# One matmul operand of an expert-mixing kernel moves by 192 bytes in the on-chip memory

## The reference, cut to what matters

```python
act = gelu(einsum('td,tkd->tk', x, u[e]))
out = einsum('tk,tkd->td', g * act, v[e])
```

## Time and profile before

| what | value |
|---|---|
| time, median of 3 runs | 1453.61 us (1453.2 to 1453.62) |
| profiled execution: span, first to last instruction | 1448.3 us |
| profiled execution: its own time | not recorded beside the span; the median is 5.3 us above the span |
| TensorE busy | 1414.5 us, 98% of the span, 7503 matmuls |
| weight loads | 1233.1 us, 85% |
| VectorE busy | 1236.6 us, 85% |
| ScalarE busy | 587.7 us, 41% |
| GpSimd busy | 557.0 us, 38% |
| moved by DMA | 402.34 MB, mean 278 GB/s |

### The profile page before, as it was taken

How to read it: one execution, slowest core, us unless ns; L and a number is a source line. 1 busy time by engine, 2 the same in 40 slices (tenths; PEclk the granted TensorE clock), 3 DMA queues, 4 the chain that set the end, 5 groups by cost and what they waited for, 6 DMA issues and landing times.

```text
span 1448.3 us, 20679 instructions
## 1 busy us (share of the span) xinstructions
PE 1414.5 (98%) x7503; PEld 1233.1 (85%) x7503; DVE 1236.6 (85%) x2019; ACT 587.7 (41%) x693; POOL 557.0 (38%) x389
## 2 busy tenths in 40 slices
PE   7999999999999999999999999999999999999997
PEld 6775478899999999898888888888888888888886
DVE  6988969999999988656788888888898888888889
ACT  3561363333335787753333333333333333333331
POOL 0100224559964000001445545454465555554500
PEclk7899999999999999999999999999999999999999
DMA  9824340025566789898999999999999999999961
GB/s 381 324 117 174 145 193 1 1 76 177 185 216 209 246 251 275 272 341 331 371 367 346 370 365 356 368 354 369 358 361 379 368 359 360 377 363 366 355 228 58
DMA packets 159326, 402.34 MB, mean 278 GB/s; under 512 B 11392, under 2 KB 79104, under 8 KB 156192
## 3 DMA queue, kind: packets, MB, share of 16 engines
q1 hardware_dynamic: 120688, 262.17, 51.2%
q0 software_dynamic: 38288, 139.08, 25.4%
q10 hardware_dynamic: 288, 0.29, 0.1%
HBM read 359.56 MB, written 41.94 MB: 277 GB/s over the span
## 4 chain that ended last, share of the span: by engine, by line
PE 66%; DVE 24%; DMA 4%; ACT 3%; issue 1%; SPq 1%; DVEq 0%; ACTq 0%
PE bank L983 21%; PE bank L984 21%; PE bank L985 20%; DMA u_raw<-ut_dram 2%; DVE arena L1598 2%; DVE arena L1590 2%; DMA wbuf<-ada_w_dram 2%; DVE arena L1595 1%; DVE arena L1587 1%; DVE arena L1639 1%; DVE arena L1592 1%; DVE arena L1640 1%; PE bank L1072 1%; DVE arena L1636 1%; PE bank L1196 1%
## 5 line engine op out<-in xcount | busy, mean ns | idle before, releaser
L983 PE MATMUL bank<-h_lo,u_hi 128*128 128x384 f32 (+1 forms) x1256 | 438.7, 349 | 1.4 <-POOL u_lo L617 1.2
L985 PE MATMUL bank<-h_hi,u_hi 128*128 128x384 f32 (+1 forms) x1256 | 433.2, 345 | 0.0
L984 PE MATMUL bank<-h_hi,u_lo 128*128 128x384 f32 (+1 forms) x1256 | 433.1, 345 | 0.0
L984 PE MATMUL bank<-v_hi,w_lo 128*128 128x512 f32 x744 | 294.5, 396 | 0.0
L983 PE MATMUL bank<-v_lo,w_hi 128*128 128x512 f32 x744 | 292.1, 393 | 0.3 <-DVE w_lo L1736 0.3
L985 PE MATMUL bank<-v_hi,w_hi 128*128 128x512 f32 x744 | 290.4, 390 | 0.0
L983 PEld LDWEIGHTS bank<-h_lo,u_hi 128*128 128x128 f32 x1256 | 236.1, 188 | 14.1 <-issue 2.0
L984 PEld LDWEIGHTS bank<-h_hi,u_lo 128*128 128x128 f32 x1256 | 236.2, 188 | 11.3 <-issue 0.5
L877 ACT ACTIVATE v_hi<-v_raw 128x2048 fp32r<-128x2048 f32 x62 | 119.0, 1919 | 312.4 <-PE bank L985 301.8
L985 PEld LDWEIGHTS bank<-h_hi,u_hi 128*128 128x128 f32 x1256 | 236.0, 188 | 9.4
L1730 DVE TENSOR_TENSOR v_lo<-v_raw,v_hi 128x2048 fp32r<-128x2048 f32 x62 | 142.8, 2304 | 110.2 <-ACT v_hi L877 108.7
(11 more groups left out here) (246 smaller groups left out, 1814.6 us busy)
## 6 DMA issues: line engine op xcount, KB each, us to landing
u_raw<-ut_dram SPq DMA_DIRECT2D x128, 512.0 KB, 6.1
v_raw<-v_dram SPq DMA_DIRECT2D x64, 1024.0 KB, 7.3
gate_in<-gates_dram SPq DMA_DIRECT2D x64, 384.0 KB, 7.2
wbuf<-ada_w_dram SPq DMA_DIRECT2D x6, 2048.0 KB, 11.1
early_dram<-arena SPq DMA_DIRECT2D x64, 192.0 KB, 2.1
gates_dram<-wbuf SPq DMA_DIRECT2D x3, 4096.0 KB, 16.3
w_raw<-early_dram SPq DMA_DIRECT2D x64, 192.0 KB, 5.5
wbuf<-ada_w_dram SPq DMA_DIRECT2D x8, 1024.0 KB, 15.8
```

Source lines behind the costliest of these rows:

```text
L983: pe.matmul(out, a_hi, b_lo, start=(k == 0), stop=False)
L984: pe.matmul(out, a_lo, b_hi, start=False, stop=False)
L985: return pe.matmul(out, a_hi, b_hi, start=False, stop=(k == n - 1))
```

## The change

`gap1` grows by 48 floats and `gap2` shrinks by 48. `w_lo` between them begins 192 bytes further up; all behind `gap2` stays in place.

```diff
         w_hi = sb("w_hi", [P, 2, 2, SD], F32R)
-        sb("gap1", [P, 720])
+        sb("gap1", [P, 768])
         w_lo = sb("w_lo", [P, 2, 2, S], F32R)
-        sb("gap2", [P, 816])
+        sb("gap2", [P, 768])
```

## The result

| | before | changed | ratio, 95% interval |
|---|---|---|---|
| first comparison, median us | 1453.57 (5 runs) | 1445.65 (5 runs, 1443.53 to 1447.15) | 0.9946 [0.9934, 0.9958] |
| second comparison (first experiment), median us | 1450.82 (19 runs) | 1446.76 (8 runs) | 0.9972 [0.9960, 0.9983] |
| profiled executions, span us | 1448.3 and 1447.2 | 1443.9 and 1442.5 | |

Of twelve further runs of the kernel before (`again_before`) one took 3242.77 us, which no ratio here counts and nothing here explains. What the change did is best seen in the loop of 60 pairs, which is the same to 0.01 us in both profiles of each kernel.

What follows compares the result with a forecast made beforehand. TensorE's matmul steps were taken to bound the loop: 60 value blocks, each 0.15 us shorter (8.32 to 8.17), save 9.0 us, so 1453.6 - 9.0 = 1444.6 us; range 1443.8 to 1447.8.

Steps and rivals of the forecast that it cites:

- TensorE is the bound, and stays it: In the loop everybody waits for TensorE; its pair goes from 12.48 to 12.33 us, VectorE has at most 10.8 us.
- The rival on transfers: DMA engines, 0.98 to 0.99 busy, become the bound at 368 GB/s; only 1.8 us gained, 1451.8 us; chance 0.03.
- The settled step falls from 231.1 to 226.7 ns: Value matmuls of 512 columns in the loop: with w_lo at the common place, 36 steps take 8.16 us.
- no change: Rival: the value step depends on something else, such as traffic, or tiles are placed otherwise; 1453.6 us; chance 0.06.
- slower: Rival: coinciding starts of weights and stream cost time; value steps rise to 233.3 ns, 1458.4 us; chance 0.05.
- Start-up price 0.01 us per value block: First steps after the 384-column expert matmuls cost 0.01 us extra, so a block takes 8.17 us and gains 0.15.
- the nearest row: Last two pairs' matmuls after the loop, all operands at the common place, settled after three steps; basis for 9.0 us.
- the lower bound of 6.0: Gain if each value block's first 12 steps stay and only the other 24 shorten: 0.10 us per block, 6.0 us.
- The gain arrives whole: What the 60 value blocks save reaches the end whole, since the closing chain leaves TensorE with the gelu at 1397.82 us.
- 5.3 us lie around the span: Measured median 1453.61 us is 5.3 us above the profiled span of 1448.3; the change does not affect that.

Runs made afterwards that it cites:

- first experiment: Kernel before and changed kernel run once more, files unchanged: medians 1450.82 us (19 runs) and 1446.76 us (8 runs), ratio 0.9972.
- again_before: The kernel before, run again with nothing changed: median 1450.37 us over all 12 runs, ratio 0.9999 to the kernel before.
- the wide kernel: Changed kernel with the expert matmuls of 48 pairs over 512 token columns instead of 384, the added columns not read: 1505.69 us.

## Why the prediction was right, and which term was off

- *TensorE is the bound, and stays it.* Right: no wait in the loop after but the 0.3 us at its start, at 367 and 372 GB/s. The rival on transfers is refuted; 368 was no ceiling.
- *The settled step falls from 231.1 to 226.7 ns.* Right, with 5.44 us for 24 steps. The rival "no change" fell with it, and "slower" too: of eight places of the weights, none has shorter steps than the one where starts coincide.
- *Start-up price 0.01 us per value block.* This is the term that was mis-sized. It is 2.76 - 2.72 = 0.04 us in the value block, and another 0.026 us in the expert block (4.186 against 24 x 173.33 = 4.160), which the prediction left at 4.16 us. The kernel before paid next to nothing at these places: its first 12 value steps take 2.774 us, 12 of its settled ones 2.772, and its expert block 4.163. The change itself brought the price, for which the prediction had no row. I had called the closing set the nearest row, because it too followed steps with w_lo off. But it follows steps of its own column count; what costs is the change from 384 to 512 columns and back, as the wide kernel shows. So a pair gains 0.0935 us and not 0.15, and the loop 5.6 us and not 9.0. That is even below the lower bound of 6.0, since the bounds let only the value block vary.
- *The gain arrives whole.* For the loop it does; the chain behind it starts from the same gelu. The load of x in that chain took 4.87 us and not 6.14. In three other kernels with the changed kernel's loop time (weights 256 bytes off) it took 6.0 to 6.5, so I take this for chance; no run settles it.
- *5.3 us lie around the span.* Wrong, without harm to the difference. Time and span of one execution are 1.8 us apart (1445.65 and 1443.9; 1448.98 and 1447.2 in the second profile of before). The profiled execution of before was some 3.5 us quicker than the median that I set beside it.
- *1444.6 us, 1443.8 to 1447.8.* 1445.65 lies inside, but by luck: with the 5.6 us that the loop gives, the forecast would have been 1448.0, above the range. If the loop is in the timed runs what it is in the profiles, the other 2.3 us of the first comparison come from the parts ahead of it and behind it, not from the sum. In the second comparison, against its own 1450.82 us, the gain of 4.1 us is under the lower bound of 6.0.

## What to carry to other kernels

Where TensorE is the bound and operands are 32 bits wide, read steps (start to start) by kind of matmul from the timeline, and compare kinds of equal columns: a few ns between them can be the place of a tile, mended with a gap of some bytes. Blocks that alternate between two column counts pay again at each change, so look at the first dozen steps of a block by themselves, and at the block behind the one that you changed. For a gain of 0.4%, take the verdict from the stretch that the change acts on, when the rest of the kernel varies by as much from run to run.

## What the runs showed of the hardware that was not expected

- The step of a matmul depends on where its weights begin, modulo 256 bytes, with the streams left in place: 226.7 ns at equal places, 228.9 to 234.0 at the seven others, for 512 columns; for 384 columns 173.3 at 0 and at 192, 176.0 to 176.7 at 128, 160 and 224 in the loop. The Trainium skill ("TensorE: Matmul & The Clock Gate", section "Step-by-step: what each phase is for") says that loading weights takes no read bandwidth from the running matmul. By that alone their place should not matter, and in these runs it does; what carries the effect, no run shows.
- At the 2.4 GHz level 128 columns more cost 226.7 - 173.3 = 53.4 ns, 0.417 a column. By that rate 512 and 384 columns are 213.3 and 160.0 ns; at equal places both counts stand 13.3 ns above, and no place tried brought that down. At the 1.2 GHz level nothing stands above: the 320.0 ns of 384 columns in the fall of the clock are twice 160.0, and with u 192 and 224 bytes off such steps take 320 too.
- A change of the column count from 384 to 512 costs 41 ns over nine steps, and back again 26 ns over six, with all operands at equal places. With w_lo off, the two cost some 5 ns together; with w_hi off instead, the way back costs 28. What in TensorE carries this from step to step is open.
